# Strassen stages: high weights over both parts of the activations at once in three of seven products, with two shared PSUM banks

## The reference

```
h = rms_norm(x); proj = h @ w_in                      # q, k, v of two attentions
gates = sigmoid(h @ w_gate + b_gate)                  # 2048 -> 4096
merged = g_diff * (oa @ w_branch_diff) + g_fox * (ob @ w_branch_fox)
x = x + merged @ w_out
u = relu(rms_norm(x) @ w_mlp_up)                      # 2048 -> 8192
x = x + (u * u) @ w_mlp_down                          # 8192 -> 2048
```

## Time and profile before

| | us |
|---|---|
| median of 3 runs | 2651.12 (2649.47 to 2651.6) |
| the profiled execution: its time | 2650.83 |
| the profiled execution: its span | 2649.0 |
| TensorE busy, matmuls | 2627.5 |
| VectorE busy | 1919.8 |
| ScalarE busy | 1212.4 |
| GpSimd busy | 86.1 |

### The profile page before, as it was taken

How to read it: one execution, slowest core, us unless ns; L and a number is a source line. 1 busy time by engine, 2 the same in 40 slices (tenths; PEclk the granted TensorE clock), 3 DMA queues, 4 the chain that set the end, 5 groups by cost and what they waited for, 6 DMA issues and landing times.

```text
span 2649.0 us, 45964 instructions
## 1 busy us (share of the span) xinstructions
PE 2627.5 (99%) x18028; PEld 2449.6 (92%) x18028; DVE 1919.8 (72%) x2712; ACT 1212.4 (46%) x1587; POOL 86.1 (3%) x134
## 2 busy tenths in 40 slices
PE   9999999999999999999999999999998999999999
PEld 8999998888888888888899999999998999999999
DVE  4648885566666634435588888888888888888887
ACT  5534443555555532223454444444454444444444
POOL 1000000000000000000000000000000000000000
PEclk9999999999999999999999999999999999999999
DMA  7444444333333345444445455444465666666654
GB/s 254 115 134 128 127 130 128 95 89 88 88 84 89 87 128 143 143 134 144 143 140 169 168 172 194 160 152 158 145 236 165 194 183 174 170 181 180 183 195 132
DMA packets 370074, 392.32 MB, mean 148 GB/s; under 512 B 22024, under 2 KB 341512, under 8 KB 369424
## 3 DMA queue, kind: packets, MB, share of 16 engines
q1 hardware_dynamic: 341680, 312.00, 38.4%
q0 software_dynamic: 8784, 30.96, 5.1%
q10 hardware_dynamic: 19472, 47.46, 4.7%
HBM read 323.20 MB, written 67.13 MB: 147 GB/s over the span
## 4 chain that ended last, share of the span: by engine, by line
PE 95%; DVE 3%; DMA 1%; ACT 1%; issue 0%; SPq 0%; ACTq 0%; DVEq 0%
PE job L2247 4%; PE job L2251 4%; PE job L2249 4%; PE scores L2251 4%; PE scores L2247 4%; PE scores L2249 4%; PE job L1958 3%; PE job L1961 3%; PE job L1960 3%; PE stats L2247 2%; PE stats L2251 2%; PE stats L2249 2%; PE job L2153 2%; PE turned L2251 2%; PE turned L2249 2%; PE turned L2247 2%
## 5 line engine op out<-in xcount | busy, mean ns | idle before, releaser
L970 ACT ACTIVATE hi<-pair 128x1792 fp32r<-128x1792 f32 x268 | 456.4, 1703 | 714.4 <-PE heads_out L2251 340.7
L1556 DVE TENSOR_TENSOR lo<-pair,hi 128x1792 fp32r<-128x1792 f32 x268 | 542.5, 2024 | 143.1 <-ACT hi L970 142.6
L1272 DVE TENSOR_TENSOR w_lo<-raw,w_hi 128x512 fp32r<-128x512 f32 x284 | 195.5, 689 | 194.0 <-ACT w_hi L780 150.8
L2247 PE MATMUL scores<-h,hi 128*128 128x256 f32 x1024 | 290.4, 284 | 5.6 <-DVE lo L1556 5.6
L2247 PE MATMUL job<-h,hi 128*128 128x256 f32 x1016 | 288.8, 284 | 6.7 <-DVE lo L1556 6.7
L2251 PE MATMUL scores<-h,lo 128*128 128x256 f32 x1024 | 289.8, 283 | 0.0
L2249 PE MATMUL scores<-h,hi 128*128 128x256 f32 x1024 | 289.7, 283 | 0.0
L2251 PE MATMUL job<-h,lo 128*128 128x256 f32 x1016 | 287.9, 283 | 0.0
L2249 PE MATMUL job<-h,hi 128*128 128x256 f32 x1016 | 287.8, 283 | 0.0
L780 ACT ACTIVATE w_hi<-raw 128x512 fp32r<-128x512 f32 x160 | 101.0, 632 | 251.8 <-PE job L1961 133.1
L2247 PEld LDWEIGHTS job<-h,hi 128*128 128x128 f32 x1016 | 195.3, 192 | 8.0 <-issue 7.8
(11 more groups left out here) (557 smaller groups left out, 7171.0 us busy)
## 6 DMA issues: line engine op xcount, KB each, us to landing
pair<-in_w_mlp_up SPq DMA_DIRECT2D x256, 256.0 KB, 2.8
pair<-in_w_mlp_down SPq DMA_DIRECT2D x248, 256.0 KB, 3.2
h<-u_rows SPq DMA_DIRECT2D x39, 896.0 KB, 7.4
raw<-in_w_in SPq DMA_DIRECT2D x256, 128.0 KB, 2.5
u_rows<-u_blocks ACTq DMA_DIRECT2D x32, 896.0 KB, 4.2
pair<-in_w_gate SPq DMA_DIRECT2D x72, 256.0 KB, 3.0
raw<-in_w_out SPq DMA_DIRECT2D x64, 256.0 KB, 3.3
sum_rows<-blocks POOLq DMA_DIRECT2D x21, 512.0 KB, 8.7
```

The lines of the kernel that those rows point to most:

```text
L970: nc.scalar.activation(pair_hi[j % 2], pairs[j][:, :, 1:8], ACT.Copy).then_inc(pair_hi_ready, 1)
L1272: nc.vector.tensor_tensor(lo, raw[:, slot, part:part + KU], hi.bitcast(F32), ALU.subtract).then_inc(split_ready, 1)
L1556: nc.vector.tensor_tensor(pair_lo[j % 2], pairs[j][:, :, 1:8], pair_hi[j % 2].bitcast(F32), ALU.subtract).then_inc(pair_lo_ready, 1)
L2247: nc.tensor.matmul(into, high, slice_of(s, a, 0), start=first, stop=False, skip_group_check=True)
```

## The change

Three of the seven products (P1, P2 and P6; activations and weights number 0, 2 and 5) send high weights over the high and the low half of the activations in one matmul of 512 columns, and low weights over the high half in one of 256 columns, added to the second half of the bank. Such a product fills a whole bank: its first half holds high x high, its second the two other terms. The halves are added afterwards. For this P1 takes the first bank of the group's set, and P2 and P6 take the banks wide and heads_out, which are now **shared** by both sets. The other four products stay as they were. The high and low buffers of the activations become halves of one tensor, so that both can be addressed at once.

New on ScalarE: `copy_shared` copies the second halves of both shared banks (2 x 256 columns) to SBUF, one group later in step m = 0 or 4 (j = 0), behind the rounding; P1's copy now takes the second half of its bank. New on VectorE: `fold_shared` adds the first halves to that copy, also in m = 0 or 4 behind the split and ahead of the pair sum; and P1's two halves are added as the first step of the early combine. New waits on TensorE: the shared products of the last unit (j = 3) come first in it, those of the first unit (j = 0) last, behind a wait for the previous group's shared fold. The first up group's fourth unit waits for all eight slices at its start.

Core of the diff:

```diff
+            wide, heads_out = shared[:, 0], shared[:, 1]
...
-                nc.scalar.activation(parts[0][:, 2], bank_sets[b][3][:, 0:2 * P], ACT.Copy).then_inc(p1_copied, 1)
+                nc.scalar.activation(parts[0][:, 2], bank_sets[b][0][:, 2 * P:S], ACT.Copy).then_inc(copied, 1)
+
+            def copy_shared(p, blocks):
+                act.wait_ge(shared_done, p + 1)
+                if not (isinstance(p, int) and p == 0):
+                    act.wait_ge(c_first, p)
+                nc.scalar.activation(blocks[:, 6:8], shared[:, :, 2 * P:S], ACT.Copy).then_inc(copied, 1)
...
+            def fold_shared(p, blocks):
+                dve.wait_ge(copied, p * 2 + 1)
+                nc.vector.tensor_tensor(blocks[:, 6:8], shared[:, :, 0:2 * P], blocks[:, 6:8],
+                                        ALU.add).then_inc(folded, 1)
...
-                p2_p6, p4_p5, p7_p3 = map(halves_of, bank_sets[b][0:3])
-                dve.wait_ge(p1_copied, p + 1)
+                p4_p5, p7_p3 = map(halves_of, bank_sets[b][1:3])
+                dve.wait_ge(copied, p * 2 + 2)
+                nc.vector.tensor_tensor(blocks[:, 2], bank_sets[b][0][:, 0:2 * P], blocks[:, 2],
+                                        ALU.add).then_inc(folded, 1)
+                dve.wait_ge(folded, p * 2 + 2)
...
                     if not (first and m < 2):
                         split_pair(n, m % 4, pairs_g, pair_hi_g, pair_lo_g)
+                    if m == 0 and not first:
+                        fold_shared(i * 2 - 1, blocks_g)
+                    if m == 4:
+                        fold_shared(i * 2, blocks_g)
...
+            def wide_product(into, high, low, right, first, last):
+                nc.tensor.matmul(into[:, :].rearrange("p (l s) -> p l s", l=2), high, right, start=first, stop=False,
+                                 skip_group_check=True)
+                return nc.tensor.matmul(into[:, 2 * P:S], low, right[:, 0], start=False, stop=last,
+                                        skip_group_check=True)
...
+            def up_unit(n, j, b, p, first=False, right=up_right):
+                high, low = pair_hi[j % 2], pair_lo[j % 2]
                 pe.wait_ge(pair_lo_ready, n + 1)
+                if j == 3:
+                    if first:
+                        pe.wait_ge(h2_ready, 8)
+                    shared_products(j, high, low, right).then_inc(shared_done, 1)
                 for k in range(2):
+                    if first and j < 3:
+                        pe.wait_ge(h2_ready, 2 * j + k + 1)
+                    done = set_products(b, j, k, high, low, right)
+                if j == 0:
+                    pe.wait_ge(folded, p * 2 - 1)
+                    if first:
+                        pe.wait_ge(x2_added, 16)
+                if j < 3:
+                    done = shared_products(j, high, low, right)
                 done.then_inc(pair_used, 1)
...
-            for n in (6, 0, 1, 4, 5, 2, 3):
+            for into, a, w in ((bank_sets[LAST % 2][0], 0, 0), (wide, 2, 2), (heads_out, 5, 5)):
+                for k in range(2):
+                    done = wide_product(into, high[:, k, w], low[:, k, w], down_slice(LAST + 6 + k, a), False, k == 1)
+                done.then_inc(last_done, 1)
+            for n in (2, 3, 0, 1):
```

More of the change, by code:

```diff
@@ L1017, in _ @@
                 gate_pairs(i)
-            for n in range(LEAD + 1):
+            round_qk(0)
+            copy_shared(GATE_PAIRS - 1, blocks_g)
+            for n in range(1, LEAD + 1):
                 round_qk(n)
@@ L1181, in up_pairs @@
                         round_pair(n, m % 4, n - 1)
+                    if m == 0 and not first:
+                        copy_shared(i * 2 + (GP - 1), blocks)
+                    if m == 4:
+                        copy_shared(i * 2 + GP, blocks)
                     if m == 1 and not first:
@@ new lines, in set_products @@
+            def set_products(b, j, k, high, low, right):
+                wide_product(bank_sets[b][0], high[:, k, 0], low[:, k, 0], right(2 * j + k, 0),
+                             j == 0 and k == 0, j == 3 and k == 1)
+                for a, w, bank, half in in_set:
+                    into = bank_sets[b][bank][:, 2 * P * half:2 * P * (half + 1)]
+                    both, first = right(2 * j + k, a), j == 0 and k == 0 and half == 0
+                    nc.tensor.matmul(into, high[:, k, w], both[:, 0], start=first, stop=False, skip_group_check=True)
+                    nc.tensor.matmul(into, high[:, k, w], both[:, 1], start=False, stop=False, skip_group_check=True)
+                    done = nc.tensor.matmul(into, low[:, k, w], both[:, 0], start=False, stop=(j == 3 and k == 1),
+                                            skip_group_check=True)
+                return done
@@ new lines, in shared_products, with gate_right @@
+            def shared_products(j, high, low, right):
+                for a, w, bank in in_shared:
+                    for k in range(2):
+                        done = wide_product(shared[:, bank], high[:, k, w], low[:, k, w], right(2 * j + k, a),
+                                            j == 0 and k == 0, j == 3 and k == 1)
+                return done
+            def gate_right(s, a):
+                if a < 3:
+                    return a_both[:, :, s + HALF * (a > 0), late if a != 1 else early]
+                return c_both[:, :, s, (0, 2, 1, 3)[a - 3]]
@@ L2094, in gate_unit @@
[L2094 to L2102 removed]
+                    done = set_products(b, j, k, high, low, gate_right)
```

159 lines of the change are left out of this document (85 added, 74 removed).

## The result

The changed kernel takes 2658.51 us (median of 7 runs, 2656.01 to 2659.02), the kernel before 2650.89 (7 runs, 2647.77 to 2651.6): the ratio is 1.0029, with a 95% interval of 1.002 to 1.0039. It is 7.6 us slower. The sum was off by little and one term by much.

A forecast was written before the change was run, and what follows sets the result against it. TensorE, busy 99% of the span, was taken to bound the kernel. Joins' gain of 23.9 us against added costs summed to -0.5 us, giving 2650 us, called the same within 5.3 us; range 2641 to 2663.

The forecast's parts named there:

- the price of a join: TensorE, Strassen stages: joining two 256-column matmuls saves 13.1 ns, 1824 joins 23.9 us.
- gates' lateness: Gate stage: VectorE's late splits make TensorE wait, 0.96 us in each of 11 groups, 10.5 us.
- scalings: Eight groups with the scalings of x2: splits come late, 0.53 us each, 4.2 us.
- sums of squares: Second up pair: a 0.60 us sum of squares in each of four units delays splits, 0.8 us.
- totals: Last seven groups with a total: splits come late, 0.47 us each, 3.3 us.
- first up group: Its fourth unit waits for the eighth slice at its start: 1.5 us later, 0.3 of gain not had, 1.8 us.
- start of the down stage: VectorE's queue is the path there and both folds lie on it, five units' gain not had: 1.5 us.
- end: End of the kernel: copy and fold come after the last shared product, 1.1 us.
- gates' first unit: It waits for the value stage's last copies sooner in the sequence: 0 to 0.6 us, taken as 0.2.
- Rival one: Lateness stays below the slack outside the gates; only gates and one-off places cost: 2642 us, chance 0.24.
- Rival two: Down stage: weights come late, all 31 groups stall at 0.4 us each: 2663 us, chance 0.12.
- Rival three: Joins do not pay: two-run operand streams at 239.8 ns, units stay 5.04 us: 2666 us, chance 0.06.

The follow-up runs named there:

- e14: e12 with each 512-column matmul again cut into two of 256 columns: 2654.51 us.
- e2: The changed kernel with each 512-column matmul again cut into two of 256, banks, folds, waits and order kept: 2667.81 us.
- e5: The changed kernel with low partners widened to 512 columns and the merge stage's high x low matmul cut into two of 256: 2821.47 us.
- e8: The changed kernel with the scaling of x2 moved from a pair's unit 5 to unit 7: 2656.49 us.
- e4: The changed kernel with the next unit's weights rounded and split ahead of copying and combining block products in the gate stage: 2669.2 us.
- e9: e6 with ScalarE's wait for the multiplied gates and the two sigmoids moved behind its rounding of unit 3's weights: 2653.96 us.
- e12: The changed kernel with e9, e7, e8, one more gate-stage sum moved, and the last groups' totals behind the next unit's split: 2643.53 us.
- e6: e4 with the gate scaling and one sum of weights moved behind the split of unit 2: 2710.36 us.
- e7: The changed kernel with the seventh slice's products first in the first up group's fourth unit, so the eighth slice is awaited later: 2656.46 us.

## Why the prediction was wrong

**The step that failed is the price of a join**, "joining two 256-column matmuls with the same weights saves 239.8 - 226.7 = 13.1 ns". The 226.7 was read where 512-column matmuls follow only each other; here each stands ahead of a narrow one. The text bounded the operand's layout and took the lower bound; the neighbour it did not bound at all. In its place: 6.7 ns by the unit, 6.0 by e14, 5.1 by e2 (the three agree within their intervals), so 9 to 12 us of gain instead of 23.9. e5 shows the reason: mixed widths. By the rule of the Trainium skill for isolated matmuls ("TensorE: Matmul & The Clock Gate", Back-to-back issue gap) the joins would give 4.6 us, an estimate from its 2.5 ns a matmul. That is too little: the measured gain lies between it and the rows.

The other terms, as predicted and as the trace has them:

| term | predicted | measured | from |
|---|---|---|---|
| joins | -23.9 | -9 to -12 | unit 5.00, e2, e14 |
| gates' lateness | 10.5 | 8.5 | 11 x 0.77 |
| scalings | 4.2 | 2.8 | e8: 322.8 to 320.0 |
| sums of squares | 0.8 | 0.5 | units 8 to 16 of the up stage: 41.37 in place of 41.17, and 0.32 of gain not had |
| totals | 3.3 | 2.7 | 7 x 0.38 |
| first up group | 1.8 | 3.2 | 3.05 later and 0.16 of gain not had; 1.5 of it the clock |
| start of the down stage | 1.5 | 1.5 | +1.3 by unit starts and 0.2 |
| end | 1.1 | 1.6 | by unit starts |
| gates' first unit | 0.2 | 0.2 | 5.19 in place of 5.00 |

- *VectorE's lateness was right in kind and place* (e4, e8, e9 and e12 take its stalls away by order alone): the chained distance of 6.51 against 6.52, stalls in the second and third unit of 11 groups, eight in the scaling groups, seven in the last, one of some microseconds in the first up group. Those in the queues of the three stages are a little smaller than I had them, since a unit lasts 5.00 and not 4.96 and so leaves 0.04 to 0.08 more room, and TensorE started 0.06 behind a split's end in the gate stage where the earlier trace rows gave 0.15.
- *The gates grew by 6.7 us as forecast* (10.5 - 3.8 = 6.7) because two errors met: stalls 8.5, units' gain 1.9. A stage's total that agrees doesn't prove its terms.
- *The first up group cost more than its price*, 3.2 in place of 1.8, though the wait was foreseen to 0.02 us. What no term had was the granted clock of 0.50 for 3.4 us behind that wait, 1.5 us of cost; without it (e6's execution) the term would be 1.7. e7 takes the idleness away, and the clock stays.
- *Rival one* (lateness hidden outside the gates) fell: stalls in all places named. *Rival two* (transfers late in the down stage) fell: fewer transfer waits than before in this execution. *Rival three* was nearest in what it said one would see, starts 0.24 apart, and wrong in its mechanism: the up stage's operand is one run of 512 columns and has the same pitch as the gates' two runs, and the narrow ones behind are shorter. Its price, 2666, is that of joins that give nothing, and e2, which has none, measured 2667.8.
- *Nothing for the new wait* on the shared fold was right: no such wait appears in the trace.

With 6.7 ns a join and everything else as put, my sum would have been 2650.8 + 11.2 = 2662.0 for the profiled execution, which took 2656.0. So the small overestimates, and the late transfer that only the kernel before had, hid part of the large error: that the forecast missed by no more than 8 us is in part luck.

## What to carry to other kernels

Price a wider instruction from rows in which it stands among the neighbours that it will have; a uniform stretch of another stage gives a bound and not the value. When work is added to a queue that is nearly full (VectorE, busy 36.5 us in two gate groups whose matmuls take 40), write down for each unit when its inputs are there and when it is due, over all the engines that hand it on, before moving a block: one order cost 10.7 us, a second 52 (some 20 of them by the clock), and the third gained 4.5, of the same instructions. Keep TensorE's single waits short: one of about 3 us can cost more than its length. And a change that is slower may still be worth keeping until its queue is mended: joins and moves together gave 0.46%, where the joins' change alone lost 0.29%.

## What the runs showed of the hardware

- 512-column matmuls in a uniform row follow each other after 226.7 ns, 256-column ones after 119.9. Mixed in pairs as in the changed kernel, the wide ones take 230 to 243 (mean 236) and the narrow one behind them 113 to 120 (mean 118); a wide one with its narrow partner comes to 353.7, 7 more than the sum. The pitch is the same for an operand of one run of 512 columns (up stage) and of two runs of 256 (gates and down stage), 236 each.
- A wait of TensorE costs about 0.1 us beyond its length in the gap to its second matmul (0.33 in place of 0.24), and in the gate stage the next unit too had such a gap of 0.33 behind a wait too short for the trace to name.
- In the first up group the granted clock went to 0.50 behind an idle time of 2.8 to 3.0 us in seven traces of eight, for 3.4 us in five and 6.8 us in two; in the changed kernel it fell 1.2 us after work had begun again. Behind 0.7 to 0.9 us in the same place (seven traces) it stayed at 1.00, and so it did behind e4's ten waits of 1.5 us in the gate stage. Behind e6's 11 waits of 3.4 to 3.8 us there it was 0.50 each time.
- The same wait does not always cost the same. At the start of the down stage both kernels have two idle times of 3.3 to 3.7 us: in the kernel before the clock fell behind the second only (2006.5 to 2009.9), in the changed one behind the first only (1999.7 to 2003.1).
